# Inverse roots of three norms by ScalarE's Sqrt and a step of Heron on VectorE in place of GpSimd's power, with a new order of two stages

## The reference, cut to what matters

```
def rms_norm(x, gain, eps=1e-6):
    y = x * rsqrt(mean(x * x, axis=-1) + eps)
    return y * gain

# first block
h = rms_norm(x, pre_norm_gain)                  # norm "x"
proj = h @ w_in                                 # q, k, v, z_a, b, c, u, z_c
attn = ...                                      # differential attention, its own norm
x = x + rms_norm(mixed @ w_out, post_norm_gain) # norm "m1"
x = x + sigmoid(x @ w_ple_gate) * rms_norm(p @ w_ple_proj, ple_norm_gain)
# second block, layer A, gMLP
y = gmlp(rms_norm(x, a_pre_g)) @ a_w_out
h = x + rms_norm(y, a_post_g)                   # norm "a"
kv_in = rms_norm(h, kv_norm_g)                  # norm "h3"
k, v = kv_in @ w_k, kv_in @ w_v
# layer B, sliding window attention
q, z = split(rms_norm(h, b_pre_g) @ b_w_in)     # same root as "h3"
out = h + rms_norm(swa(q, k, v) * silu(z) @ b_w_out, b_post_g)
```

## Time and profile before

| | |
|---|---|
| median of 3 runs | 885.3 us (885.14 to 886.25) |
| the profiled execution's own time | 885.75 us |
| its span, first to last instruction | 884.0 us |
| TensorE busy | 868.2 us (98%) |
| ScalarE, VectorE, GpSimd busy | 360.3, 537.2, 542.8 us |
| mean granted TensorE clock | 0.998 |

### The profile page before, as it was taken

One profiled execution on the slowest core, in us unless ns is written; L12 is line 12 of the kernel. 1 busy time (PEld: TensorE's weight loads), 2 busy tenths in 40 slices (PEclk: granted clock), 3 DMA queues, 4 the chain that ended last, 5 costly groups with the idle time before them and its releaser, 6 DMA issues.

```text
span 884.0 us, 11936 instructions
## 1 busy us (share of the span) xinstructions
PE 868.2 (98%) x4220; PEld 722.0 (82%) x4220; DVE 537.2 (61%) x880; ACT 360.3 (41%) x804; POOL 542.8 (61%) x604
## 2 busy tenths in 40 slices
PE   8999999999999999999999999999997999999997
PEld 6888888888888787888888888888887888888886
DVE  6125648875035489775765535556996457788624
ACT  4123333431134377546112321113775536767622
POOL 7766556587789832317975038771359798566352
PEclk9999999999999999999999999999999999999999
DMA  7533231342322468885742253526962222112202
GB/s 198 167 120 96 74 92 51 96 143 92 128 90 96 124 146 177 208 203 190 162 124 95 73 190 96 125 90 152 217 180 71 72 73 93 51 49 72 73 1 95
DMA packets 81517, 102.65 MB, mean 116 GB/s; under 512 B 11826, under 2 KB 54322, under 8 KB 81459
## 3 DMA queue, kind: packets, MB, share of 16 engines
q1 hardware_dynamic: 72752, 85.12, 30.1%
q0 software_dynamic: 8704, 16.78, 11.2%
q10 hardware_dynamic: 2, 0.00, 0.0%
HBM read 99.79 MB, written 2.10 MB: 115 GB/s over the span
## 4 chain that ended last, share of the span: by engine, by line
PE 88%; POOL 4%; DVE 2%; DMA 2%; ACT 2%; issue 1%; POOLq 0%; DVEq 0%; ACTq 0%
PE bank L2076 26%; PE bank L2078 26%; PE bank L2077 26%; PE bank L2319 2%; PE bank L2347 1%; PE bank L2173 1%; DMA gain<-in_a_w_in 1%; DVE wlo L1667 1%; POOL wlo L850 1%; PE bank L2292 1%; PE bank L2342 1%; PE bank L2341 1%; DMA raw<-in_a_w_in 1%; POOL ms L795 1%; POOL whi L841 1%
## 5 line engine op out<-in xcount | busy, mean ns | idle before, releaser
L850 POOL TENSOR_TENSOR wlo<-raw,whi 128x512 fp32r<-128x512 f32 x204 | 280.4, 1404 | 0.7 <-ACT whi L972 0.7
L841 POOL TENSOR_SCALAR whi<-raw 128x512 fp32r<-128x512 f32 x202 | 140.8, 733 | 188.1 <-PE bank L2078 179.1
L2076 PE MATMUL bank<-actB_hi,whi 128*128 128x512 f32 (+1 forms) x416 | 159.6, 384 | 0.6 <-POOL wlo L850 0.6
L2077 PE MATMUL bank<-actB_lo,whi 128*128 128x512 f32 (+1 forms) x416 | 158.7, 381 | 0.0
L2078 PE MATMUL bank<-actB_hi,wlo 128*128 128x512 f32 (+1 forms) x416 | 158.5, 381 | 0.0
L2076 PE MATMUL bank<-whi,actA_hi 128*128 128x512 f32 x318 | 125.9, 396 | 1.2 <-DVE actA_lo L1421 0.7
L2078 PE MATMUL bank<-whi,actA_lo 128*128 128x512 f32 x318 | 124.0, 390 | 0.0
L2077 PE MATMUL bank<-wlo,actA_hi 128*128 128x512 f32 x318 | 123.9, 390 | 0.0
L2076 PEld LDWEIGHTS bank<-actB_hi,whi 128*128 128x128 f32 x416 | 78.3, 188 | 15.4 <-issue 1.1
L2078 PEld LDWEIGHTS bank<-actB_hi,wlo 128*128 128x128 f32 x416 | 78.2, 188 | 15.2
L2077 PEld LDWEIGHTS bank<-actB_lo,whi 128*128 128x128 f32 x416 | 78.3, 188 | 14.1
(11 more groups left out here) (269 smaller groups left out, 1579.4 us busy)
## 6 DMA issues: line engine op xcount, KB each, us to landing
raw<-in_a_w_in SPq DMA_DIRECT2D x44, 512.0 KB, 4.2
raw<-in_w_in SPq DMA_DIRECT2D x32, 512.0 KB, 3.9
raw<-in_b_w_in SPq DMA_DIRECT2D x16, 512.0 KB, 3.4
raw<-in_a_w_out SPq DMA_DIRECT2D x12, 512.0 KB, 3.3
gain<-in_a_w_out POOLq DMA_DIRECT2D x9, 512.0 KB, 8.2
raw<-in_w_out SPq DMA_DIRECT2D x8, 512.0 KB, 3.4
raw<-in_w_ple_gate SPq DMA_DIRECT2D x8, 512.0 KB, 3.3
gain<-in_a_w_in POOLq DMA_DIRECT2D x8, 512.0 KB, 7.7
```

Source lines behind the costliest of these rows:

```text
L841: pool.tensor_scalar(H, src[:, i * HALF:(i + 1) * HALF], 1.0, 1.0, ALU.mult, ALU.mult).then_inc(w_hi, 1)
L850: ins = pool.tensor_tensor(L, src[:, i * HALF:(i + 1) * HALF], H.bitcast(f32), ALU.subtract)
L2076: M(out_, whi_, xhi_, start=start, stop=False)
L2077: M(out_, whi_, xlo_, start=False, stop=False)
```

## The change

For the norms x, a and h3 the root leaves GpSimd. With m the mean square over 4 plus epsilon over 4, ScalarE takes s = Sqrt(m) and VectorE makes 1/(m/s + s): Heron's step for the root of m, whose missing division by 2 makes the result the inverse root of 4m. The squares are scaled by 1/64 in place of 1/32 for it. Each root is on ScalarE one small Identity that adds epsilon to the first sum (`add_eps`; none for x 0 and x 1, one for a 0 and a 1 together, one for a 2 and a 3) and one small Sqrt with the other sum (`std`), and on VectorE four instructions of one column (`inverse`): an addition, a reciprocal, a scalar-tensor-tensor, a reciprocal. A Sqrt on a spare column stands ahead of each stage so that the function table is loaded there. The other norms keep GpSimd's root.

The order changes too. Start: ScalarE squares x 1 before it copies the first transposes, VectorE puts the inverse of x 1 before `rest x 0 0` and `normed_x(1)` before `rest x 0 1`. Junction: TensorE transposes n 0 between A(13,0) and A(13,1), and v5 t waits for the first remainder at its start and for the second at its matmul 13. VectorE does `h3_in(0)` before the second half of `lo_a(13)`. ScalarE divides the scaling of k5's second half around `h3_out(0)`. GpSimd's queue keeps the splits alone, in their old order.

```
+            def std(name, t, c, done):
+                n = NORMS[name]
+                if name == "x" and t < 2:
+                    act.wait_ge(x_squared, t + 1)
+                else:
+                    act.wait_ge(std_step, STD_STEP["eps", name, t // 2 * 2 if name == "a" else t])
+                act.wait_ge(squared[name], done)
+                A(rstd[:, n, t:t + 1], ss[:, n, t, c:c + 1], ACT.Sqrt, bias=ms[:, n, t:t + 1]).then_inc(std_step, 1)
+            def inverse(name, t):
+                n, c = NORMS[name], ROOTED_LAST[name, t]
+                nth = 3 * next(inverses)
+                last, mean, first, sum_ = (ss[:, n, t, k:k + 1] for k in (c, 1 - c, 2, 3))
+                root = rstd[:, n, t:t + 1]
+                dve.wait_ge(std_step, STD_STEP[name, t])
+                V.tensor_tensor(mean, last, ms[:, n, t:t + 1], ALU.add).then_inc(root_step, 1)
+                V.reciprocal(first, root).then_inc(root_step, 1)
+                dve.wait_ge(root_step, nth + 2)
+                V.scalar_tensor_tensor(sum_, mean, first, root, ALU.mult, ALU.add).then_inc(root_step, 1)
+                dve.wait_ge(root_step, nth + 3)
+                V.reciprocal(root, sum_).then_inc(rstd_ready[name], 1)
...
-            after[0] = [lambda: root("x", 1, D)]
-            after[0.5] = [lambda: root("x", 2, D)]
-            after[1] = [lambda: root("x", 3, D)]
-            after[at("v5", 0, 1) - 0.25] = [lambda: root("a", 0, D), lambda: root("a", 1, D)]
-            after[at("v5", 0, 1)] = [lambda: root("h3", 0, D)]
-            after[at("k5", 0, 0) - 0.5] = [lambda: root("h3", 1, D)]
-            after[at("k5", 0, 1) - 0.5] = [lambda: root("a", 2, D)]
-            after[at("k5", 0, 1)] = [lambda: root("a", 3, D), lambda: root("h3", 2, D)]
-            after[at("q5", 0, 0) - 0.5] = [lambda: root("h3", 3, D)]
...
             square_x(0)
+            inverse("x", 0)
             normed_x(0)
             square_x(1)
+            inverse("x", 1)
             rest("x", 0, 0)
+            normed_x(1)
             rest("x", 0, 1)
-            normed_x(1)
             rest("x", 1, 0)
+            inverse("x", 2)
             normed_x(2)
...
             lo_a(13, (0,))
             part_gain(0, 1)
+            inverse("a", 0)
+            h3_in(0)
             lo_a(13, (1,))
             part_gain(1, 1)
-            h3_in(0)
+            inverse("a", 1)
+            inverse("h3", 0)
             h3_in(1)
             add_kept(6, 0, p03_kept(0), a_out_(2, 0), (c7_made, 28 + 6))
+            inverse("h3", 1)
+            rest("n", 0, 0)
+            rest("n", 0, 1)
             add_kept(6, 1, p03_kept(1), a_out_(3, 0), (c7_made, 28 + 10))
-            rest_n(0)
             part_gain(2, 0)
-            rest_n(1)
+            inverse("a", 2)
+            rest("n", 1, 0)
             h3_in(2)
+            rest("n", 1, 1)
             part_gain(3, 0)
+            inverse("a", 3)
+            inverse("h3", 2)
             h3_in(3)
+            inverse("h3", 3)
...
-    o += turn("n", 0) + turn("n", 1) + [("v5", 0), ("v5", 1)]
+    assert o.pop() == ("A", 13, 1)
+    o += turn("n", 0) + [("A", 13, 1)] + turn("n", 1) + [("v5", 0), ("v5", 1)]
```

More of the change, by code:

```diff
@@ L802, in root_attn @@
                 pool.tensor_scalar(ms_attn[:, h, :], ss_attn[:, h, :], 1.0 / DV1, SUBLN_EPS, ALU.mult, ALU.add)\
[L803 to L804 removed]
+                    .then_inc(ms_ready, 1)
+                pool.wait_ge(ms_ready, next(roots))
                 pool.tensor_tensor(r_attn[:, h, :], ms_attn[:, h, :], mhalf[:, 0:1].to_broadcast([P, T]), ALU.pow)\
@@ L967, in square_x, with add_eps, std_x @@
                     square("x", t, c, resid[:, t, c * HALF:(c + 1) * HALF])
+            def add_eps(name, t, tiles, c, done):
+                n = NORMS[name]
+                act.wait_ge(squared[name], done)
+                A(ms[:, n, t:t + tiles], ss[:, n, t:t + tiles, c], ACT.Identity, bias=eps[:, 0:1]).then_inc(std_step, 1)
+            def std(name, t, c, done):
+                n = NORMS[name]
+                if name == "x" and t < 2:
+                    act.wait_ge(x_squared, t + 1)
+                else:
+                    act.wait_ge(std_step, STD_STEP["eps", name, t // 2 * 2 if name == "a" else t])
+                act.wait_ge(squared[name], done)
+                A(rstd[:, n, t:t + 1], ss[:, n, t, c:c + 1], ACT.Sqrt, bias=ms[:, n, t:t + 1]).then_inc(std_step, 1)
+            def std_x(t):
+                if t >= 2:
+                    add_eps("x", t, 1, 0, 2 * t - 1)
+                std("x", t, int(t >= 2), t + 1 if t < 2 else 2 * t)
             act.dma_start(gain[0:1, 1], pre_norm_gain[0:1, :]).then_inc(gain_in[0], 16)
+            act.wait_ge(consts_made, 3)
+            A(lams[:, 7:8], eps[:, 0:1], ACT.Sqrt)
             square_x(0)
+            std_x(0)
             act.wait_ge(raw_in[0], LANDED[0, 0])
             A(halves_of(0, 0, 2)[0], raw[:, 0, :], ACT.Copy).then_inc(w_hi, 2)
+            square_x(1)
+            std_x(1)
             turned("x", 0, 0)
-            square_x(1)
             turned("x", 0, 1)
             square_x(2)
+            std_x(2)
             turned("x", 1, 0)
+            turned("x", 1, 1)
             square_x(3)
-            turned("x", 1, 1)
+            std_x(3)
             for t in range(2, T):
@@ L1234, in square_a, with h3_square, h3_std @@
                 square("a", t, c, a_out_(t, c))
+            def h3_square(t, c):
+                act.wait_ge(h3_ready, 2 * t + c + 1)
+                square("h3", t, c, resid[:, t, c * HALF:(c + 1) * HALF])
+            def h3_std(t):
+                add_eps("h3", t, 1, 0, 2 * t + 1)
+                std("h3", t, 1, 2 * t + 2)
             def h3_out(t):
-                for c in range(2):
-                    act.wait_ge(h3_ready, 2 * t + c + 1)
-                    square("h3", t, c, resid[:, t, c * HALF:(c + 1) * HALF])
+                h3_square(t, 0)
+                h3_square(t, 1)
+                h3_std(t)
             def y4_hi(j):
@@ L1310, in scale_two @@
                 act.wait_ge(small_in, 16 * 13)
-                for k in range(4):
+                for k in cols:
                     w = src[:, k * 256:(k + 1) * 256]
@@ L1325, in _ @@
             square_a(1, 0)
+            act.wait_ge(consts_made, 6)
+            A(lams[:, 7:8], eps[:, 0:1], ACT.Sqrt)
             hi_a(10)
@@ L1471, in _ @@
             rest("x", 2, 0)
+            inverse("x", 3)
             normed_x(3)
```

59 lines of the change are left out of this document (38 added, 21 removed).

## The result

The changed kernel takes 894.83 us, median of 5 runs (893.76 to 896.86), against 885.78 of the kernel before, run beside it: a ratio of 1.0105, 95% interval 1.0091 to 1.012, or 9.05 us more. The prediction was 894.8. The profiled execution has a time of its own of 894.83 at a span of 893.1.

A forecast was written before the change was run, and what follows sets the result against it. TensorE is busy 98% of the span, so only its idle times count. Junction 8.5 plus start 1.0 is 9.5 on the profiled 885.75, giving 895.25; the median lies 0.45 lower, so 894.8, range 887.5 to 899.0.

The forecast's parts named there:

- Steps 1 to 3: Junction: VectorE and GpSimd take turns from lo_a(13), so its second half ends at 667.1, against 661.55 before.
- Step 4: Junction, middle of A(13,0): TensorE's seventh matmul waits for lo_a(13)'s second half, a new stall of 4.7, 1.2 from order alone.
- Step 5: Junction: four small waits of VectorE's inverses beside GpSimd's splits, 2.3 in all; inverse of h3 0 done at 672.0.
- The case in which these small instructions slip through: Rival, start and junction: inverse's small instructions never wait; start costs 0, junction 4.2 to 4.7, total 889.7; chance 0.20.
- Step 6: Junction: normed_n(0) takes 1.13, so tr n 0 comes at 673.2 against 668.46, 4.7 late.
- Step 7: Junction: A(13,1) at 2.7 and two turns of transposes at 0.85 each put v5 0 at 677.9, 5.8 late.
- The rival: Junction: granted clock falls in the stalls of 4.7, costing 1 to 3 us more, total 897; chance 0.06.
- Steps 8 and 9: Junction: v5 1 stalls 1.8 and 0.8 for its remainders; 3.0 before tr n 2, which comes at 692.0.
- Step 10: Junction's end: nothing stalls after tr n 2, v5 2 starts at 696.6 against 688.07, +8.5 (bounds +4.2 to +10.5).
- The start, +1.0: Start: inverse x 2 meets one or two wlos, so the transposes of x 2 come about 1 later; bounds 0 to 1.6.
- The faster rival: Junction: VectorE's run of instructions keeps GpSimd out until it ends; v5 2 is 3.9 early, total 881.4; chance 0.12.
- The rival of the tables: ScalarE: Square isn't in Sqrt's table, about 16 loads of 1.28, 20 us, total over 905; chance 0.02.

The follow-up runs named there:

- b_filled: Kernel before with the new junction only, plus unused matmuls filling TensorE's stalls in A(13,0) and before tr n 0: 895.52 us, ratio 1.0099 to the kernel before.
- b_hold: Changed kernel with the start of before, GpSimd's k5 splits held until h3_in 1 and q5's until h3_in 3: 885.26 us, 0.9993 to the kernel before.
- start_only: Changed kernel with the junction of the kernel before, so only the start is new: 888.53 us, ratio 1.0034 to the kernel before.
- start_one_tensor: New start, junction of before, inverse's addition and scalar-tensor-tensor rewritten with one tensor operand: 886.24 us, ratio 1.0008 to the kernel before.
- b_one_tensor: Changed kernel with the start of before, inverse's addition and scalar-tensor-tensor rewritten with one tensor operand: 891.12 us, ratio 1.0051 to the kernel before.

## Why the prediction was right, by its steps

The forecast of 894.8 met 894.83, by the mechanism that it named: turns between GpSimd's splits, freed of the roots' pauses, and VectorE's instructions. That it met the second digit is luck: terms were off in both directions, one rival came in beside it, and the runs of after alone spread over 3.1.

- Steps 1 to 3, the order worked out in turns. `part_gain` ended at 661.1 (661.5 predicted), inverse a 0 at 662.1 (662.2), k5's `whi` began at 661.3 (661.4), the second half of `lo_a(13)` ended at 666.9 (667.1), all less the 1.27.
- Step 4, the stall of 4.7: 4.48. Its part from the order alone, put at 1.2 and called certain, is 1.85 with k5 and q5 held and 0.46 with v5's `wlo` held as well, so it too is in good part a matter of turns.
- Step 5: the additions and scalar-tensor-tensors of the inverses of a 1 and h3 0 waited 0.41, 0.25, 0.99 and 0.89 beyond their plain 0.15 and 0.22, 2.5 against the 2.3 taken. The case in which these small instructions slip through is refuted. ScalarE's small instructions are 0.28 and 0.30 for the 0.3 taken. In the form with one tensor they slip through and the time falls by about 3 us.
- Step 6: tr n 0 at 672.6 (673.2).
- Step 7 failed in its size: v5 0 at 679.4, not 677.9. The clock had fallen. By the durations above that is 0.74 for the transposes and 1.70 for A(13,1), 2.4 in all, less the 0.6 by which tr n 0 was early and the 0.3 by which the forecast had tr n 1 wait for its tile. The rival gave this 0.06 and made it a case of its own; it happened, and together with the forecast.
- Steps 8 and 9: stalls of 0.24 and 0.75 for 1.8 and 0.8, and 1.53 for 3.0. In all they were 3.1 smaller, about 1.5 of it because TensorE came that much later; tr n 2 at 691.2 (692.0) waits for VectorE's and ScalarE's lists. So the mistake of step 7 fell into stalls that the forecast had anyway. It was not foreseen, and `b_filled` shows that removing it moves the lists too.
- Step 10, +8.5: 7.7 in after's profile, and 0.86% or 7.6 us for the junction alone (8.2 between the medians). The cause, turns with GpSimd, is shown by `b_hold`: 0.9993.
- The start, +1.0 with bounds 0 to 1.6: 1.27 in after's profile, but 3.2 in the median alone, outside the bounds. This is the term that was mis-sized. I had counted the inverses and missed that the square of x 1 reads two operands as well, that its landing decides whether it waits, and that in the new order ScalarE's copies wait for it (0.96 in `start_only`, 1.09 in `start_one_tensor`). In the order of before the first copy of x 0 stands ahead of this square on ScalarE; a run of before in which the square met the `wlo` was not seen.
- The faster rival, VectorE keeping GpSimd out, is refuted: GpSimd had its turn between the two halves of `h3_in` (663.72). The rival of the tables is refuted by the five loads.
- The Trainium skill ("SBUF — State Buffer", SBUF: two separate sides) says that a two-input VectorE op and a GpSimd op that reads SBUF shut each other out of a shared pair of SBUF ports for a whole instruction. The trace agrees, down to one column: 1.16 at most.

## What to carry to other kernels

Taking work off an engine removes pauses that another engine may have been living on. Before a root or a copy leaves GpSimd, list which of VectorE's next instructions read two tensors from SBUF and lie on the way to TensorE; hold the splits behind them by a semaphore, or write the small ones with one tensor operand and columns of scalars. Of a stall ask whether others follow it: in `b_one_tensor` the stall of 4.47 stayed, and the kernel was still 3 us faster. And before you put a small instruction ahead of an engine's copies, ask what it waits for.

## What the runs showed that I had not expected

- A tensor_scalar instruction with its second and third operand as columns of SBUF never waited: 0.195 to 0.214 and 0.272 to 0.275 in eight each, in a stage where the two-tensor form took up to 1.17 for the same value.
- The turns make time out of a landing: whether a tile arrived 0.1 before or 0.2 after a split's start made 1 us on one instruction (0.71 or 1.65), and so did a weight that landed 1.1 later (1.77). The runs spread over 4.0 us; with the split held, over 1.7.
- Keeping TensorE's clock up in one stall moved its fall to a later one (690 to 700 at 0.83), and the junction took 2.1 us longer in the profile.
